# A block's operand rests and half of its weight rests moved to VectorE, and modulation's sum moved ahead of the block

## What is computed

```python
    # first block, behind the scans of its mixer
    h = h * head_norm * sigmoid(o)          # output gates
    x = x + h @ w_out                       # projection
    x = x + square(relu(rmsnorm(x, norm_mlp) @ w1)) @ w2     # feed-forward, D_FF = 4096
    ...
    # second block
    mod = silu(c) @ ada_w + ada_b           # 1 x 1024 times 1024 x 3072
    shift, scale, gate = split(mod, 3)
    h = rms_norm(x, norm_g) * (1 + scale) + shift
```

## Time and profile before

| what | value |
| --- | --- |
| time, median of 3 runs (lowest, highest) | 2500.0 us (2496.4, 2501.08) |
| the profiled execution: time, span | 2503.78 us, 2502.0 us |
| TensorE busy in the span | 2376.1 us, 95% |
| VectorE, ScalarE, GpSimd busy | 66%, 40%, 48% |
| output gates (327 to 430 us), projection (to 507.5) | 103.0 and 77.5 us |
| feed-forward block (507.5 to 1175.6) | 668.1 us |
| of it phases 0 to 7 | 97.7, 79.1, 77.1, 86.8, 77.1, 86.8, 77.1, 86.4 us |

### The profile page before, as it was taken

The page is one execution under the profiler, slowest core; times in us unless marked ns, Lnnn a source line. Parts: engine busy times, 40 slices in busy tenths (PEclk is TensorE's granted clock), DMA queues, the critical chain, the costliest instruction groups (busy, mean ns, idle before and its releaser), DMA issues. The chain is left out here.

```text
span 2502.0 us, 42282 instructions
## 1 busy us (share of the span) xinstructions
PE 2376.1 (95%) x17029; PEld 1918.0 (77%) x17029; DVE 1643.0 (66%) x2393; ACT 1013.0 (40%) x1723; POOL 1193.6 (48%) x690
## 2 busy tenths in 40 slices
PE   7998999998999999998999989999999998988998
PEld 6887878876887878877878657787786668887886
DVE  6112543289769678487667399999997764555842
ACT  4213553354343343344453266445333662214231
POOL 3221334477847658468664226456362202321774
PEclk9999999999999999999999999999999998999999
DMA  3112413155543633412224402342243001003423
GB/s 141 51 44 76 143 35 110 51 202 210 219 151 110 246 128 142 182 68 68 76 69 135 151 20 89 102 133 88 100 135 143 27 19 61 29 29 127 154 84 110
DMA packets 92466, 266.50 MB, mean 107 GB/s; under 512 B 9544, under 2 KB 22896, under 8 KB 85104
## 3 DMA queue, kind: packets, MB, share of 16 engines
q1 hardware_dynamic: 85360, 251.21, 29.3%
q10 hardware_dynamic: 6912, 12.59, 1.4%
HBM read 214.85 MB, written 49.95 MB: 106 GB/s over the span
## 5 line engine op out<-in xcount | busy, mean ns | idle before, releaser
L326 POOL TENSOR_TENSOR weights_lo_in_place<-wbuf,weights_hi_by_slot 128x1024 fp32r<-128x1024 f32 x130 | 322.6, 2485 | 488.4 <-ACT weights_hi_by_slot L322 488.1
L332 PE MATMUL ps<-region_rounded,weights_hi_by_slot 128*128 128x512 f32 x1280 | 509.7, 398 | 19.6 <-DVE region_rounded L654 14.1
L334 PE MATMUL ps<-region_rounded,weights_lo_in_place 128*128 128x512 f32 x1280 | 500.3, 391 | 0.0
L333 PE MATMUL ps<-region_rounded,weights_hi_by_slot 128*128 128x512 f32 x1280 | 499.9, 391 | 0.0
L332 PEld LDWEIGHTS ps<-region_rounded,weights_hi_by_slot 128*128 128x128 f32 x1280 | 241.5, 189 | 79.5 <-issue 26.1
L333 PEld LDWEIGHTS ps<-region_rounded,weights_hi_by_slot 128*128 128x128 f32 x1280 | 241.7, 189 | 52.1 <-issue 3.4
L334 PEld LDWEIGHTS ps<-region_rounded,weights_lo_in_place 128*128 128x128 f32 x1280 | 241.3, 189 | 50.8
L1430 PE MATMUL ps<-region_rounded 128*128 128x512 f32 x448 | 180.0, 402 | 25.4 <-DVE region_rounded L1956 23.9
L322 ACT CAST weights_hi_by_slot<-wbuf 128x1024 fp32r<-128x1024 f32 x130 | 134.9, 1044 | 154.1 <-DMA wbuf<-w_o 47.8
L1430 PE MATMUL ps<-region_rounded,weights_hi_by_slot 128*128 128x512 f32 x448 | 176.9, 395 | 7.3 <-DVE region_rounded L1956 6.0
L1432 PE MATMUL ps<-region_rounded 128*128 128x512 f32 x448 | 177.8, 397 | 0.0
(11 more groups left out here) (423 smaller groups left out, 5066.1 us busy)
## 6 DMA issues: line engine op xcount, KB each, us to landing
region_rounded<-scratch_mlp_lo SPq DMA_DIRECT2D x21, 1024.0 KB, 4.9
region_rounded<-scratch_mlp_hi SPq DMA_DIRECT2D x21, 1024.0 KB, 5.1
wbuf<-w_hn SPq DMA_DIRECT2D x37, 512.0 KB, 4.1
wbuf<-w_mlp SPq DMA_DIRECT2D x32, 512.0 KB, 6.4
region<-w_mlp SPq DMA_DIRECT2D x32, 512.0 KB, 6.1
wbuf<-w_in SPq DMA_DIRECT2D x25, 512.0 KB, 3.9
region<-xT SPq DMA_DIRECT2D x24, 512.0 KB, 7.0
xtra<-w_ada SPq DMA_DIRECT2D x48, 256.0 KB, 5.7
```

What stands on the lines that cost most here:

```text
L326: self.nc.gpsimd.tensor_tensor(self.m.lo4[:, n % SLOTS, :], self.m.raw4[:, n % SLOTS, :], self.m.hi4[:, n % SLOTS, :].bitcast(F32), ALU.su ...
L332: nc.tensor.matmul(out, m.hi4[:, s, w], m.rounded(hi + k, half(hf)), start=(k == 0), stop=False)
L333: nc.tensor.matmul(out, m.hi4[:, s, w], m.rounded(lo + k, half(hf)), start=False, stop=False)
L334: return nc.tensor.matmul(out, m.lo4[:, s, w], m.rounded(hi + k, half(hf)), start=False, stop=(k == KT - 1))
```

## The change

All operand rests of the block go to DVE (both even and odd quarters), and of the weights' rests those of odd products: `weights_lo` on DVE, four products ahead, behind `operand_lo` in each iteration. POOL keeps the weight rests of even products. ACT rounds quarters 2 and 3 of P2 before the loop, and DVE makes all four rests of P2 there. The 48 steps of modulation move from phases 0 to 5 into units 2 to 13 of gates and projection, four behind each unit; their buffers move, there are six sums `acc` now, and the columns are summed in two batches of 12 matmuls, behind unit 8 and unit 14. SP starts four pieces per unit, between the loads of weights. Line numbers of the order after are those of the changed kernel: 1966 is the operand rest, 1976 the weight rest on DVE, 2031, 2048 to 2051 and 2059 are 2011, 2028 to 2031 and 2039 of before, 1986 and 1990 are 1966 and 1970, 2086 is a step of modulation.

The core of the diff:

```diff
--- before.py
+++ after.py
...
 MP = PHASES * PER_PHASE
-RING, HI_LEAD, SUM_LEAD, OP_HI_LEAD, OP_LO_LEAD = 8, 5, 6, 6, 4
+RING, HI_LEAD, SUM_LEAD, OP_HI_LEAD, OP_LO_LEAD, W_LO_LEAD = 8, 5, 6, 6, 4, 4
...
 OG_EARLY = 2
+ADA_FIRST = 2
...
                                    m.rounded(OX + k).bitcast(F32), ALU.mult, ALU.subtract).then_inc(m.o_lo, 1)
+def wait_weights_lo(mlp, eng, s):
+    q = s % 2
+    eng.wait_ge(mlp.w_lo[q], mlp.w_lo_0[q] + s // 2 + 1)
...
     mlp.op_hi, mlp.op_hi_0 = g_hi, 2 * KT
-    mlp.op_lo, mlp.op_lo_0 = [g_lo, g_lo_last], [2 * LO_LAST, 2 * (KT - LO_LAST)]
+    mlp.op_lo, mlp.op_lo_0 = g_lo_last, 2 * (KT - LO_LAST)
+    mlp.w_lo, mlp.w_lo_0 = [mlp.w_lo_even, g_lo], [0, 2 * LO_LAST]
...
     S2 = [m.tmp[:, 6 + hf, :] for hf in range(2)]
-    acc = [m.tmp[:, 6 + q, :] for q in range(2)]
-    stage = [m.xtra[:, q * ADA_COLS:(q + 1) * ADA_COLS] for q in range(3)]
+    acc = [m.tmp[:, 6, :], m.tmp[:, 7, :], m.tmp[:, 2, :], m.xtra[:, 0:HALF], m.xtra[:, HALF:T], m.tmp[:, 6, :]]
+    stage = [m.xtra[:, T:T + ADA_COLS], m.tmp[:, 0, :], m.tmp[:, 1, :]]
...
         return i % KT, i // KT
+    def ada_pieces(n):
+        return range(4 * (n - ADA_FIRST), 4 * (n - ADA_FIRST) + 4) if ADA_FIRST <= n < ADA_FIRST + PIECES // 4 else range(0)
...
                     sp.wait_ge(ada_added, i - 2)
+                elif i:
+                    sp.wait_ge(h_squared, NC * MH)
...
                     load_top(0, o)
+                    if o == 0:
+                        for i in ada_pieces(P0 - SLOTS + 1):
+                            ada(i)
...
                     load_low(0, o)
-                for i in range(3):
-                    ada(i)
...
                             store_operand(i + 1)
-                        for q in ((i,) if i < P4 else (i, i + 1)):
-                            if KT * f + 3 + q < PIECES:
-                                ada(KT * f + 3 + q)
...
                         sp.dma_start(m.chunk(TX + k), m.d["xT"][k]).then_inc(x_loaded[k], 16)
+                for i in ada_pieces(n - SLOTS + 1) if n < P0 else ():
+                    ada(i)
...
-            def ada_columns(c):
-                pe.wait_ge(ada_added, KT * (c + 1))
-                pe.wait_ge(mlp.taken, taken_before(c + 1) - 2 * PAIRS + 1)
-                for t in range(4):
-                    ins = nc.tensor.matmul(m.ps[:, PAIRS, t:t + 1], acc[c % 2][:, t * P:(t + 1) * P], m.const("ones")[:, 0:1],
-                                           start=True, stop=True)
+            def ada_columns(q):
+                pe.wait_ge(ada_added, 3 * KT * (q + 1))
+                if q == 0:
+                    pe.wait_ge(h_gated, 2 * KT)
+                else:
+                    pe.wait_ge(mod_steps, 1)
+                for c in range(3):
+                    for t in range(4):
+                        ins = nc.tensor.matmul(m.ps[:, PAIRS, 4 * c + t:4 * c + t + 1], acc[3 * q + c][:, t * P:(t + 1) * P],
+                                               m.const("ones")[:, 0:1], start=True, stop=True)
...
                 full(n, GH_T, GL_T, gated_ready if n == W0 else None)
+                if n == W0:
+                    ada_columns(0)
+                if n == P0 - 2:
+                    ada_columns(1)
...
                 if is_split(f):
-                    pe.wait_ge(mlp.op_lo[k % 2], mlp.op_lo_0[k % 2] + 2 * split_before(f, i) + k // 2 + 1)
+                    pe.wait_ge(mlp.op_lo, mlp.op_lo_0 + PAIRS * split_before(f, i) + k + 1)
...
                         token_sums(6 + hf, S1[hf]).then_inc(summed, 1)
-                if 1 <= f <= 6 and i == P1 and o == 1:
-                    ada_columns(f - 1)
-                if 1 <= f <= 6 and i == P2 and o == 0:
-                    pe.wait_ge(mod_steps, f)
...
             weights_hi(3)
+            operand_hi(6)
+            operand_hi(7)
...
                 f, i, o = where(s)
+                if s % 2:
+                    return
...
                 nc.gpsimd.tensor_tensor(mlp.ring_lo(s), mlp.weights_raw(s), mlp.ring_hi(s).bitcast(F32), ALU.subtract
-                                        ).then_inc(mlp.w_lo, 1)
-            def operand_lo(t):
-                f, i, o = where(t)
-                if not is_split(f) or o % 2:
-                    return
-                wait_operand_used(mlp, pool, f, i, o)
-                pool.wait_ge(mlp.op_hi, mlp.op_hi_0 + PAIRS * split_before(f, i) + o + 1)
-                nc.gpsimd.tensor_tensor(mlp.lo(f, i, o), mlp.raw(f, i, o), mlp.hi(f, i, o).bitcast(F32), ALU.subtract
-                                        ).then_inc(mlp.op_lo[0], 1)
+                                        ).then_inc(mlp.w_lo[0], 1)
...
                     add_square(2 * n + hf, J_W, x_squared, x_added)
-                if n == W0 + 6:
-                    for t in range(PAIRS):
-                        operand_lo(t)
...
             for s in range(MP):
-                operand_lo(s + OP_LO_LEAD)
...
                 f, i, o = where(t)
-                if not is_split(f) or o % 2 == 0:
+                if not is_split(f):
...
                 nc.vector.tensor_tensor(mlp.lo(f, i, o), mlp.raw(f, i, o), mlp.hi(f, i, o).bitcast(F32), ALU.subtract
-                                        ).then_inc(mlp.op_lo[1], 1)
+                                        ).then_inc(mlp.op_lo, 1)
+            def weights_lo(s):
+                f, i, o = where(s)
+                if s % 2 == 0:
+                    return
+                dve.wait_ge(mlp.w_hi, mlp.w_hi_0 + s + 1)
+                if i == P5:
+                    dve.wait_ge(mlp.summed, sums_made(f, P6, o))
+                nc.vector.tensor_tensor(mlp.ring_lo(s), mlp.weights_raw(s), mlp.ring_hi(s).bitcast(F32), ALU.subtract
+                                        ).then_inc(mlp.w_lo[1], 1)
...
+            def ada(i):
+                k, c = ada_piece(i)
+                to = acc[c]
+                dve.wait_ge(ada_loaded[i % 3], 16 * (i // 3 + 1))
+                if k == 0:
+                    if c == 5:
+                        dve.wait_ge(ada_turned, 1)
+                    nc.vector.tensor_scalar(to, stage[i % 3], m.cact[:, 0:1], None, ALU.mult).then_inc(ada_added, 1)
+                else:
+                    dve.wait_ge(ada_added, i)
+                    nc.vector.scalar_tensor_tensor(to, stage[i % 3], m.cact[:, k:k + 1], to, ALU.mult, ALU.add).then_inc(ada_added, 1)
+            def mod_columns(q):
+                dve.wait_ge(ada_turned, q + 1)
+                nc.vector.tensor_tensor(m.mod[:, 12 * q:12 * q + 12], m.ps[:, PAIRS, 0:12], m.pars("ada_b")[:, 12 * q:12 * q + 12],
+                                        ALU.add).then_inc(mod_steps, 1)
...
                     gate_heads(f)
-            for f in range(LO_LAST, KT):
-                rest_of_last_heads(f)
+                if n == W0 - 1:
+                    for f in range(LO_LAST, KT):
+                        rest_of_last_heads(f)
+                for p in ada_pieces(n):
+                    ada(p)
...
                     sum_inputs(k - 1)
+                if n == W0 + 1:
+                    mod_columns(0)
+                if n == P0 - 1:
+                    mod_columns(1)
+                for p in ada_pieces(n):
+                    ada(p)
...
                         operand_lo(t)
+                if n == P0 - 1:
+                    weights_lo(1)
...
             sum_inputs(KT - 1)
-            def ada(i):
-                k, c = ada_piece(i)
-                to = acc[c % 2]
-                dve.wait_ge(ada_loaded[i % 3], 16 * (i // 3 + 1))
-                if k == 0:
-                    if c >= 2:
-                        dve.wait_ge(ada_turned, c - 1)
-                    nc.vector.tensor_scalar(to, stage[i % 3], m.cact[:, 0:1], None, ALU.mult).then_inc(ada_added, 1)
-                else:
-                    dve.wait_ge(ada_added, i)
-                    nc.vector.scalar_tensor_tensor(to, stage[i % 3], m.cact[:, k:k + 1], to, ALU.mult, ALU.add).then_inc(ada_added, 1)
-            def mod_columns(c):
-                dve.wait_ge(ada_turned, c + 1)
-                nc.vector.tensor_tensor(m.mod[:, 4 * c:4 * c + 4], m.ps[:, PAIRS, 0:4], m.pars("ada_b")[:, 4 * c:4 * c + 4], ALU.add
-                                        ).then_inc(mod_steps, 1)
+            operand_lo(PAIRS)
+            operand_lo(PAIRS + 1)
+            weights_lo(3)
+            operand_lo(PAIRS + 2)
+            operand_lo(PAIRS + 3)
...
                     root_inverse(1)
-                if 1 <= f <= 6 and i == P1 and o == 2:
-                    mod_columns(f - 1)
...
                         sum_hidden_last(e, u)
-                if s + OP_LO_LEAD < MP:
+                if 2 * PAIRS <= s + OP_LO_LEAD < MP:
...
                     operand_lo(s + OP_LO_LEAD)
-                if f < 6 and o == 0:
-                    ada(KT * f + i)
-                if f < 6 and i == P4 and o == 2:
-                    ada(KT * f + KT - 1)
+                if s + W_LO_LEAD < MP:
```

(5 more changed lines are left out.)

22 lines of the change are left out of this document (12 added, 10 removed).

## The result

The changed kernel takes 2482.8 us at the median of four runs beside 2500.2 of the kernel before on the same chip, a ratio of 0.9925 with a 95% interval of 0.9905 to 0.9945: a small gain, but clear of no change. In two later sets of runs it came to 0.9895 (0.9873 to 0.9917) and 0.9899 (0.9881 to 0.9917). 2480 was forecast, with a range of 2462 to 2495.

A forecast was written before the change was run, and what follows sets the result against it. PE, busy 95%, bounds the kernel, so only its waits, mostly for DVE's operand rests, can be won: 10.7 + 2.0 + 1.3 + 1 + 5.7 - 0.5 = 20.2 us off 2503.8, 2483.6, or 2480 for a median; range 2462 to 2495.

The forecast's parts named there:

- The price of a POOL instruction: DVE's queue at the turn to phase 3: each POOL instruction beside it costs DVE 0.76 us.
- Phases 3 and 5: Start of both phases: one wait of 2.8 us in place of 2.56 + 3.45; 5.4 us won each, 10.7 together.
- Phase 7: That phase of the block: 2.0 us won at its start (6.3 to 0), 1.3 in its later waits.
- Phase 0, start: Block's beginning: P2's wait goes, P5 is late instead, product 1 waits 0.7 to 1.8 us; 1 us won.
- Phase 0, end, and phase 1: P7 of phase 0 to P2 of phase 1: 6.2 us lost in place of 11.9, 5.7 won (9 to 1).
- In front: Gates and projection: PE hides modulation's steps, column sums cost 0.24 us each wherever they stand; 0.5 us lost.
- A: Feed-forward block: each POOL instruction holds DVE up for its full 1.27 us; gain 8 us, 2492; chance 0.1.
- the prediction's paragraph on the port: SBUF port: DVE and POOL contend, but not for a whole instruction, since 1.80 and 1.74 us are under 1.94.
- B: Feed-forward block: the waits go but for the start of phase 0; 43.9 us won, 2456; chance 0.12.
- C: Feed-forward block: DVE becomes the bound if its mean instruction stays at 0.91 us; 25 us lost, 2525; chance 0.08.
- D: Before the block: blocked DVE misses its bank, or column sums wait for step 24; 3 to 8 us, 2486; chance 0.08.
- E: DVE's order: it waits for ACT's rounded weights each second product, gain lost in short waits; 2500; chance 0.06.

The follow-up runs named there:

- weights on DVE: Changed kernel with all weights' rests of the block on DVE, none on POOL: 2473.9 us, ratio 0.9878.
- rests alone: Kernel before with the rests divided as in the change, modulation left in the block: 2487.8 us, ratio 0.9941.
- weights on POOL: Changed kernel with all weights' rests on POOL: 2482.7 us, ratio 0.9921.
- modulation alone: Kernel before with only modulation moved to gates and projection, all rests where they were: 2504.3 us, ratio 1.0008.
- POOL twice: Changed kernel with POOL making the even weights' rests of P1, P2, P6 and P4 twice, DVE's queue unchanged: 2504.9 us, ratio 1.0002.
- two experiments on its order: Changed kernel with the first odd weights' rest made earlier, 2478.1 us; changed kernel with P5's operand rests eight products ahead, not four, 2478.3 us.
- the kernel with the batches half a unit earlier: Changed kernel with column sums in six batches of four, the last three half a unit before their later place: 2482.1 us, ratio 0.9909.

## Why the prediction was right, point by point

**The price of a POOL instruction** was taken as 0.76 us. The queues at the turn, laid side by side (an instruction of DVE 0.605 us, 0.35 once; a POOL instruction that an end of the stretch cuts counts by its share):

| kernel | DVE | POOL | took | left for POOL | each |
|---|---|---|---|---|---|
| weights on DVE | 32 | 0 | 19.71 | 0 | |
| changed | 29 | 3 | 20.07 | 2.2 | 0.72 |
| rests alone | 31 | 3 | 21.18 | 2.1 | 0.69 |
| weights on POOL | 27 | 6.4 | 21.16 | 4.5 | 0.70 |
| modulation alone | 25 | 8.3 | 22.66 | 7.2 | 0.87 |
| before | 27 | 9.3 | 24.80 | 8.1 | 0.87 |
| POOL twice | 32 | 8 | 26.15 | 6.4 | 0.80 |

The price is right on average and wrong as a constant, for the reason that the single rows gave. An instruction of POOL costs DVE 1.1 us where the next two of DVE have both inputs in SBUF (one runs as POOL's starts, the other waits for POOL's whole instruction), 0.3 to 0.5 where one that reads PSUM goes in between, and some 0.7 where POOL's starts beside a PSUM reader. In the changed kernel's queue the three cost 0.37, 1.09 and 0.69 us over what the held instructions take alone, 2.2 together, which is the table's; in the kernel before nine held instructions make 7.9 of its 8.1. That 0.76, a mean over one mix of such cases, held for another mix was in part luck.

The rest of an operand (line 1966) shows it in one row, minimum, median and maximum in ns, beside the earlier trace rows:

```profile
L1966 DVE TENSOR_TENSOR region_rounded<-region,region_rounded x140: 673/684/1784, 505.9 to 1136.2; 128x512 fp32r<-128x512 f32 x140
```

The same work has nearly the minimum and maximum of before (674 and 1803), but a median of 684 ns where it was 1635: it is seldom held up by POOL now. Its mean is 0.84 us, near the 0.8 that was named as a sign.

**Phases 3 and 5**: 10.7 us forecast, 14.8 measured (10.6 less 0.95 of column sums is 9.7 lost before in each; now 2.3). The mechanism was right and the size off: quarter 3 was put at 21.0 us of queue with four POOL instructions, and it took 20.07 with three, so PE waited 1.54 us (1.9 from start to start) and not 2.8; and the clock's 1.2 us mostly did not come. Of the signs, "one wait of about 3 us" at the start of phases 3, 5 and 7 was so oversized, and these phases took 78.5, 78.5 and 80.0 us and not 80.5 each. Quarter 1's wait is gone, as forecast.

**Phase 7**: 2.0 at the start and 1.3 later forecast; 2.6 (4.2 where the clock held) and 3.6 measured (1.8 where one wait came). POOL's part in the later waits was underrated.

**Phase 0, start**: 1 us forecast, 1.0 measured: P1, P2 and P5 lost 11.7 us and lose 10.7 (11.9 and 10.9 in the repetitions). P2's wait went, P5's came, and product 1 waits 1.76, the top of its 0.7 to 1.8. The two experiments on its order show why the sum hardly moved: DVE's work bounds it.

**Phase 0, end, and phase 1**: 5.7 forecast, 6.7 measured (11.9 to 5.2).

**In front**: 0.5 us forecast beside 5.7 of column sums that "cost 0.24 us each wherever they stand"; measured 7.2, and 7.0 to 10.4 by units in the three executions. This is the step of the prediction that failed, by 1 to 4 us: it put the clock behind the column sums at nothing. A batch of twelve is 2.84 us, as counted, but behind the first the clock fell to its half level in unit 9 each time (1.5 to 1.7 us), and behind the second in one execution of three. DVE's part was right: blocked until 446 forecast, until 444.16 measured, and PE did not wait for a bank. The row of DVE's wait for the piece:

```profile
DVE xtra L2083 <- DMA xtra<-w_ada: 9.2, 1, 9.2
```

**The sum** was 20.2 us from the profiled execution: 26.6 came, 4.1 more at the turns, 2.9 in phase 7, 1.0 in phase 1, less 1.0 in front and 0.6 behind the block. Between medians it was 17.4, 28.4 and 25.7 us in the three sets of runs. So 20 was near for one and low for two, and that the first median came within 3 us of 2480 is in part luck: the profiled execution won 6 us more than the sum.

**The rivals.** A falls as a price: no queue gives over 0.87 us for each POOL instruction, where it wanted 1.27. Its mechanism does not fall, and the prediction's paragraph on the port read the rows wrongly. It took 1.80 and 1.74 us, both under the sum of 1.94, for a sign that neither engine holds the other off for a whole instruction. But the held DVE instruction always ends 0.55 us after POOL's, and POOL's 1.12 to 1.17 after DVE's: they take turns, and the durations stay under the sum because the first 0.1 us or so of an instruction overlaps with the end of the other's (an estimate from 0.67 less 0.55 and 1.27 less 1.15). So the rule of the Trainium skill (SBUF — State Buffer, Who interferes with whom) that the shared pair of ports is an exclusive lock fits these traces. The page says "for the whole instruction" of DVE's two-port modes, and of an instruction with two SBUF inputs that it contends; here such an instruction waits for the whole of POOL's too. What kept the price under A's is that DVE would have spent 0.605 us on its next instruction anyway (1.15 + 0.55 - 0.605 = about 1.1 us at most for one of POOL's), and that DVE's PSUM readers pass. So a hold of the whole instruction gives the 0.7 to 0.9 us of the table in this kernel, and not the 1.27 that rival A put down to it.

B and C fall by the queues; D came in part, as the clock's fall behind the columns and not as a wait, and as a wait in the kernel with the batches half a unit earlier; E had no sign in the trace.

## What to carry to other kernels

When DVE and POOL share work on SBUF, cost an instruction on POOL as DVE time too: here 0.7 to 0.9 us each on average, more than the 0.6 us it takes DVE to do the same work itself, so the helper engine is only worth using where DVE is idle or is busy with instructions that read PSUM (0.3 to 0.5 us; no run here arranged its order for that). Look at what stands next in DVE's queue, and not only at the mean. Find a point at which the engine that sets the pace last waited and use it as a ruler: count its instructions and the neighbour's from there, and the wait follows to a few tenths. Where an engine's amount of work bounds a stretch, moving a late item earlier only moves the wait; take work (or contention) away first, and reorder then.

## What the runs showed of the hardware

- A DVE instruction with both inputs in SBUF and a POOL instruction took turns: in fourteen traces all 1211 held DVE instructions ended 0.54 to 0.56 us after a POOL instruction's end. None of the 1119 DVE instructions that read PSUM beside POOL was held (0.69 us at most).
- A batch of twelve one-column matmuls (2.84 us) between full ones was followed by the half clock (1.2 GHz) in unit 9 in nine traces of nine (3.4 us of it, once 6.8), and behind unit 14 in four of the nine. Three batches of four (0.95 us each) within 14 us were followed by none, in three traces of three.
- The clock's falls did not repeat from one execution to the next: of the fourteen traces, nine lose some 2.7 us to a fall at the start of the gates, two half of that and three nothing, with the same instructions on PE and a wait of 3.3 to 3.8 us in front in all of them; behind the same wait of 1.9 us it fell in some executions and not in others. Among the 101 executions of the later sets of runs the mean granted clock goes with two thirds of the variance between executions of one kernel.
- 61 repeated instructions of POOL cost some 24 us of the whole time, an estimate from ratios on different chips (1.0002 where the changed kernel has 0.990); the block alone took 659.0 us for 633.5 to 636.0.
